# Attention of a one-core transformer kernel: projection blocks, sums of squares and key norms are placed anew over the steps

## Chip, cores and metric

The kernel runs as one program on one core of one Trainium2 chip. The metric is the device time of one execution in microseconds. The median of the runs counts.

## What is computed

The reference is a stack of two networks on one sequence of 512 tokens and 1024 channels. The first has two layers of convolution and retention. The second puts 16 meta tokens ahead (528 rows), runs a state-space layer and an MLP, then a multi-head latent attention (MLA) layer and an MLP. Only the MLA layer is touched:

```python
def mla_mixer(h, w_in, q_a_g, w_q_b, kv_a_g, w_kv_b, q_norm_g, k_norm_g, w_out):
    q_lat, kv_lat, k_pe = jnp.split(h @ w_in, [MLA_Q_RANK, MLA_Q_RANK + MLA_KV_RANK], axis=-1)
    q = (rms_norm_2(q_lat, q_a_g) @ w_q_b).reshape(bsz, L, MLA_HEADS, MLA_QK)
    kv = (rms_norm_2(kv_lat, kv_a_g) @ w_kv_b).reshape(bsz, L, MLA_HEADS, MLA_NOPE + MLA_V)
    k_nope, v = jnp.split(kv, [MLA_NOPE], axis=-1)
    k = jnp.concatenate([k_nope, k_pe of all heads], axis=-1)
    q = rms_norm_2(q, q_norm_g)
    k = rms_norm_2(k, k_norm_g)
    ...                                  # rotary turn of the last 32 of 96
    for s, e in blocks:                  # the 16 meta rows, then blocks of 128
        sc = jnp.einsum('bqhd,bkhd->bhqk', q[:, s:e], k[:, :e]) * scale
        p = jax.nn.softmax(jnp.where(mask, sc, -jnp.inf), axis=-1)
        outs.append(jnp.einsum('bhqk,bkhd->bqhd', p, v[:, :e]))
    return o @ w_out
```

There are 16 heads of 64 + 32 channels. Queries and keys are each divided by the root of their mean square (per head and token) before the scores.

## The kernel before

The code is written in one function for each engine, and each engine runs its instructions strictly in the order in which they are written. Engines meet only at semaphores (`wait_ge`). So the order of the calls in `pe_mla` (TensorE), `act_mla` (ScalarE) and `dve_mla` (VectorE) is the schedule.

The 16 heads are handled as 8 pairs, and a pair as 8 steps, `n` = 0 to 7: four query tiles of 128 tokens for head 0, then four for head 1. `STEPS` gives the tile order 0, 1, 3, 2, so that the scores of the four steps of a head have 144, 272, 528 and 400 key columns. The step counter over all pairs is `i`, 64 steps in all. Each step does:

- TensorE: the scores of step i with a mask matmul (`pe_scores`, L933 to L937), the transposes of the probabilities of step i-1 (`pe_turn_p`, L953, L955), and their product with V of step i-2 (`pe_times_v`, L970, L972, 64 columns each).
- VectorE: the maximum of each row of the scores and its negative, scaled (`dve_top`, L2258, L2260).
- ScalarE: the exponential (`act_exp`, L1426) and the copy of the transposed probabilities (`act_copy_pt`, L1439, L1441).

Beside the steps of a pair runs the preparation of the next two:

- Projection (`pe_pair_block`, L360): the queries and keys of a pair are a "unit" of 8 blocks of 128 x 128 weights. A block is three fp32r matmuls (high by high, low by high, high by low parts) of 512 columns; blocks 0 to 2 give the queries of head 0, 3 to 5 those of head 1, and 6 and 7, of two times 264 columns, the keys of both heads. They write banks 0, 1 and 2 to 3 of PSUM.
- `act_pair_q_squares`, `act_pair_keys`: squares of the queries, a copy of the keys with their gain (`k_raw`), squares of the keys (`k_squared`).
- Sums of squares (`pe_pair_totals`, L909, L913): four parts (two heads, two halves), each one 264-column fp32 matmul for the keys and two one-column ones for the queries, in banks 2 and 3.
- `dve_pair_mean` (L2214), `act_pair_rsqrt` (L1105, L1107: logarithm, then exponential) and three Newton parts (`dve_pair_newton`, L2225 to L2231) give the inverse roots of both heads in one tile of 1064 columns. `dve_pair_keys` (L2243, L2247) multiplies the keys of both heads by them and signals `k_done`; the first scores of the pair wait for it.
- `dve_pair_plain` (L2183) and `dve_pair_turn` (L2193, L2199, L2204) write the queries.

In the last two pairs there is no further pair to project, and blocks of the output projection stand as fillers in places named by `PLACES`. Weights come by DMA on SyncE's queue, are split on ScalarE (`act_split`) and GpSimd (`pool_low`, L340); that is not changed but for the step in which ScalarE splits.

In TensorE's loop before, the preparation sits like this:

```python
        if more and n == 2:
            pe_pair_totals(g, e, pair + 1, 0, 1)
        ...
        if project and n >= 4:
            pe_pair_block(g, e, pair + 2, (1, 2, 4, 6)[n - 4])
        ...
        if project and n == 2:
            pe_pair_block(g, e, pair + 2, 0)
        ...
        if project and n >= 5:
            pe_pair_block(g, e, pair + 2, (3, 5, 7)[n - 5])
```

## Time and profile before

| | us |
|---|---|
| median of 3 runs | 2783.66 |
| lowest, highest | 2774.49, 2784.95 |
| profiled execution | 2770.03 |
| its span, first to last instruction | 2768.2 |
| TensorE busy | 2672.4 (97%) |
| VectorE busy | 1223.6 (44%) |
| ScalarE busy | 980.4 (35%) |
| mean granted TensorE clock | 0.967 |

The attention loop runs from the first scores at 2092.5 us to the last transposes at 2365.5 us of the span. The page gives busy time by engine and, in 40 slices, the granted clock. The windows view gives for a stretch, in this order, its length, then busy time and number of instructions of TensorE, of its weight loads, of VectorE, ScalarE and GpSimd, then the granted clock (1.00 is 2.4 GHz, 0.50 is 1.2 GHz), DMA share and GB/s. The timeline gives instructions in order of time, those of one line merged, with the idle time before them and its releaser in brackets. Times and clocks of one execution stand beside a median of others, so small differences between the two mean nothing.

### The profile page before, as it was taken

Reading aid. Unit: us, or ns where it says so; the run is one execution under the profiler, and the core shown is the slowest. Engines: PE = TensorE matmul, PEld = TensorE weight load, DVE = VectorE, ACT = ScalarE, POOL = GpSimd, SP = SyncE. Lnnn points to the kernel's source line nnn. Section 1 sums busy time; section 2 is a strip of 40 time slices with the busy share of each in tenths; the row PEclk is TensorE's granted clock in tenths of the full one; section 3 lists DMA queues with packets and bytes.
Section 4 is the critical chain, followed back from the end, with each engine's and each line's share of the span. In section 5 each row is a group of like instructions: output and inputs, shape, how many; then the busy total and the mean of one; then the engine's idle time right before and its main releaser. Section 6 shows DMA issues by size and latency. Waiting matters only on the chain.

```text
span 2768.2 us, 36003 instructions
## 1 busy us (share of the span) xinstructions
PE 2672.4 (97%) x15144; PEld 2272.1 (82%) x15144; DVE 1223.6 (44%) x1649; ACT 980.4 (35%) x1479; POOL 932.2 (34%) x381
## 2 busy tenths in 40 slices
PE   7999999899999997999999999999979999999999
PEld 5777778677777777999999999999956777778887
DVE  6444442354444318688777331121244555422111
ACT  4333333433333323444444332232333444333222
POOL 3343344243443431233323334443321000254443
PEclk9999999999999998999999999999987888999999
DMA  4233332233332331221211222323210000133332
GB/s 134 86 111 93 95 109 84 62 110 93 95 101 86 101 91 39 62 62 56 62 60 58 73 84 86 94 88 92 81 54 23 24 16 15 55 107 99 92 91 92
DMA packets 61328, 215.65 MB, mean 78 GB/s; under 512 B 8176, under 2 KB 8560, under 8 KB 61168
## 3 DMA queue, kind: packets, MB, share of 16 engines
q1 hardware_dynamic: 57248, 202.05, 24.3%
q10 hardware_dynamic: 3920, 11.31, 1.3%
q8 instruction: 120, 1.97, 0.3%
q14 instruction: 40, 0.33, 0.0%
HBM read 211.24 MB, written 2.10 MB: 77 GB/s over the span
## 4 chain that ended last, share of the span: by engine, by line
PE 91%; DVE 5%; ACT 2%; issue 1%; DMA 0%; POOL 0%; ACTq 0%; DVEq 0%
PE psum L360 75%; PE psum L454 1%; PE psum L464 1%; PE psum L647 1%; PE psum L909 1%; PE psum L970 1%; PE psum L936 1%; PE psum L650 1%; PE psum L913 1%; PE psum L972 1%; PE psum L934 1%; PE psum L372 1%; PE psum L953 1%; PE psum L602 1%; DVE sb_scale L1537 1%
## 5 line engine op out<-in xcount | busy, mean ns | idle before, releaser
L340 POOL TENSOR_TENSOR sb_w_lo<-sb_w_raw,sb_w_hi 128x1024 fp32r<-128x1024 f32 x377 | 932.0, 2475 | 1813.9 <-ACT sb_w_hi L1098 1813.7
L360 PE MATMUL psum<-sb_h_hi,sb_w_hi 128*128 128x512 f32 (+1 forms) x2648 | 824.1, 353 | 48.2 <-DVE sb_h_lo L1546 32.7
L360 PE MATMUL psum<-sb_h_lo,sb_w_hi 128*128 128x512 f32 (+1 forms) x2648 | 795.5, 342 | 0.0
L360 PE MATMUL psum<-sb_h_hi,sb_w_lo 128*128 128x512 f32 (+1 forms) x2648 | 791.9, 341 | 0.0
L1098 ACT ACTIVATE sb_w_hi<-sb_w_raw 128x1024 fp32r<-128x1024 f32 x377 | 395.5, 1054 | 602.7 <-PE psum L360 458.8
L360 PEld LDWEIGHTS psum<-sb_h_hi,sb_w_hi 128*128 128x128 f32 x2648 | 459.5, 190 | 123.8 <-issue 36.5
L360 PEld LDWEIGHTS psum<-sb_h_lo,sb_w_hi 128*128 128x128 f32 x2648 | 458.1, 190 | 62.9 <-issue 7.5
L360 PEld LDWEIGHTS psum<-sb_h_hi,sb_w_lo 128*128 128x128 f32 x2648 | 458.4, 190 | 56.6
L360 PE MATMUL psum<-sb_mix_hi,sb_w_hi 128*128 128x264 f32 (+1 forms) x1424 | 421.9, 342 | 10.2 <-POOL sb_w_lo L340 5.6
L360 PE MATMUL psum<-sb_mix_lo,sb_w_hi 128*128 128x264 f32 (+1 forms) x1424 | 414.0, 336 | 0.0
L360 PE MATMUL psum<-sb_mix_hi,sb_w_lo 128*128 128x264 f32 (+1 forms) x1424 | 412.4, 335 | 0.0
L360 PEld LDWEIGHTS psum<-sb_mix_hi,sb_w_hi 128*128 128x128 f32 x1424 | 244.3, 190 | 48.2 <-issue 8.5
L360 PEld LDWEIGHTS psum<-sb_mix_hi,sb_w_lo 128*128 128x128 f32 x1424 | 243.9, 190 | 27.6
L360 PEld LDWEIGHTS psum<-sb_mix_lo,sb_w_hi 128*128 128x128 f32 x1424 | 244.1, 190 | 25.3 <-issue 0.5
L2114 DVE TENSOR_TENSOR sb_resid<-sb_resid,psum 128x528 f32<-128x528 f32 (+1 forms) x64 | 44.6, 697 | 289.9 <-PE psum L360 289.9
L2104 DVE SCALAR_TENSOR_TENSOR sb_square<-psum,sb_scale 128x528 f32<-128x528 f32 (+1 forms) x64 | 44.7, 699 | 174.9 <-PE psum L360 174.8
L1338 ACT ACTIVATE sb_scaled<-sb_square 128x528 f32<-128x528 f32 (+1 forms) x64 | 40.9, 639 | 216.6 <-DVE sb_square L2104 216.6
L1426 ACT ACTIVATE sb_p<-psum,sb_neg_top,sb_rinv 128x144 f32<-128x144 f32 (+1 forms) x64 | 40.4, 631 | 133.4 <-DVE sb_neg_top L2260 133.2
L2108 DVE TENSOR_TENSOR sb_mix_lo<-sb_scaled,sb_mix_hi 128x528 fp32r<-128x528 f32 (+1 forms) x64 | 49.0, 766 | 84.6 <-ACT sb_mix_hi L1340 84.6
L1546 DVE SCALAR_TENSOR_TENSOR sb_h_lo<-sb_resid,sb_cols,sb_h_hi 128x512 fp32r<-128x512 f32 (+1 forms) x48 | 51.7, 1078 | 49.1 <-ACT sb_h_hi L1114 48.8
L1272 ACT ACTIVATE sb_part<-psum,sb_neg_a 88x88 f32<-88x88 f32 x192 | 46.0, 329 | 67.9 <-PE psum L629 67.9
L1741 DVE TENSOR_TENSOR sb_ssq<-sb_ssq,sb_square 128x512 f32<-128x512 f32 x14 | 13.7, 979 | 127.0 <-ACT sb_square L1181 127.0
(275 smaller groups left out, 2637.7 us busy)
## 6 DMA issues: line engine op xcount, KB each, us to landing
sb_w_raw<-in_weights SPq DMA_DIRECT2D x377, 512.0 KB, 3.5
sb_decay<-in_decay ACTq DMA_DIRECT2D x16, 640.0 KB, 3.9
sb_resid<-in_x SPq DMA_DIRECT2D x4, 512.0 KB, 9.6
out<-sb_resid SPq DMA_DIRECT2D x8, 256.0 KB, 2.1
sb_table<-in_rope_table ACTq DMA_DIRECT2D x1, 264.0 KB, 3.4
sb_s<-in_positions ACTq DMA_DIRECT2D x1, 256.0 KB, 7.6
sb_cols<-in_cols ACTq DMA_DIRECT2D x1, 158.5 KB, 4.8
sb_ones<-in_ones ACTq DMA_DIRECT2D x1, 64.0 KB, 5.9
```

The source lines that it names most:

```text
L340: e.tensor_tensor(g.w_lo[:, u % 4, :], g.w_raw[:, u % 2, :], g.w_hi[:, u % 4, :].bitcast(F32), ALU.subtract).then_inc(S["w_lo"], 1)
L360: mm = e.matmul(g.psum[0:m, at + b, 0:wd], w[:, slot, P * i:P * i + m], xs[:, tile, c:c + wd], start=first and n == 0, stop=last and n == 2)
L372: mm = e.matmul(g.psum[:, 6 + b, 0:w], g.ones[:, :], g.square[:, m % 2, c:c + w], start=m == 0, stop=m == KT - 1)
L454: e.matmul(g.psum[:, 4 + j % 2, 0:WIDE1[j]], g.k[:, P * j:P * j + P], g.q[:, P * j:SEQ], start=True, stop=True).then_inc(S["scores"], 1)
L1098: e.activation(g.w_hi[:, u % 4, :], g.w_raw[:, u % 2, :], ACT.Copy).then_inc(S["w_hi"], 1)
L1272: a = e.activation(g.part[0:Q, h % 2, Q * j:Q * j + Q], g.flat(at + Q * j, Q)[0:Q], ACT.Exp, bias=g.neg_a[0:Q, j, n:n + 1])
L1338: e.activation(g.scaled[:, m % 2, c], g.square[:, m % 2, c], ACT.Square).then_inc(S["relu_sq"], 1)
L1426: e.activation(g.p[:, i % 2, 0:KEYS[t]], g.flat(at, KEYS[t]), ACT.Exp, bias=g.neg_top[:, n:n + 1], scale=g.q_scale(pair, h, t), accum_out= ...
L1546: e.scalar_tensor_tensor(g.h_lo[:, m, c], g.resid[:, m, c], g.gain(n, m), g.h_hi[:, m, c].bitcast(F32), ALU.mult, ALU.subtract).then_inc(S ...
L2104: e.scalar_tensor_tensor(part(g.square[:, m % 2, c]), product(k), 0.0, part(g.scale[:, c]), ALU.max, ALU.mult).then_inc(S["relu"], 1)
L2108: e.tensor_tensor(g.mix_lo[:, m, c], g.scaled[:, m % 2, c], g.mix_hi[:, m, c].bitcast(F32), ALU.subtract).then_inc(S["hidden"], 1)
L2114: e.tensor_tensor(r, r, product(k), ALU.add).then_inc(S["add"], 1)
```

## The change

Nothing in the arithmetic changes. The placement does:

- TensorE: every step of pairs 0 to 5 has one projection block. Blocks 0 to 5 of pair + 2 stand in steps 2 to 7, and blocks 6 and 7 in steps 0 and 1 of the pair after. The start-up does six blocks of pair 1, not eight. The four parts of the sums of squares stand at the ends of steps 3 to 6.
- Inverse roots and keys go head by head: the tiles of 1064 and 1056 columns are worked in halves of 532 and 528. Head 0 of the next pair is done in steps 5 to 7; head 1 has its mean and logarithm in step 7 and its Newton parts and keys in steps 2 and 3 of its own pair. `k_done` counts heads, and steps 0 and 4 both wait for it.
- ScalarE: the keys move from step 0 to step 2, with the squares first; the split moves from step 2 to step 1; the squares of the queries come after the exponential of step 7.
- VectorE: `dve_pair_plain` moves from step 7 to step 0 of the next pair.
- `PLACES`: 7 fillers in pair 6 (8 before), 14 in pair 7 (13 before).

```diff
@@ -92,8 +92,8 @@
-def rs_qk(pair):
-    return 34 + pair
+def rs_qk(pair, h):
+    return 34 + 2 * pair + h
@@ -885,7 +889,7 @@
     if i == 6 and pair:
-        e.wait_ge(S["mean"], rs_qk(pair - 1))
+        e.wait_ge(S["mean"], rs_qk(pair - 1, 1))
     c0, widths = (META, (SEQ,)) if i < 6 else (0, (HALF, HALF))
@@ -901,9 +905,9 @@
             e.wait_ge(S["q_squared"], pair + 1)
-            e.wait_ge(S["k_squared"], pair + 1)
+            e.wait_ge(S["k_raw"], 2 * pair + 2)
         else:
-            e.wait_ge(S["qk_mean"], pair + 1)
+            e.wait_ge(S["mean"], rs_qk(pair, 0))
     rows = slice(64 * h, 64 * h + 64)
@@ -921,8 +925,8 @@
     h, t, at = STEPS[n]
-    if n == 0:
-        e.wait_ge(S["k_done"], pair + 1)
+    if n % 4 == 0:
+        e.wait_ge(S["k_done"], 2 * pair + h + 1)
     if i == 0:
@@ -990,8 +994,8 @@
 FILLERS = [(m, n) for m in range(3) for n in range(PAIRS - 2)] + [(m, PAIRS - 2) for m in range(3)]
-PLACES = [(NS * (PAIRS - 2) + n, at) for n, at in ((2, 1), (4, 0), (5, 0), (5, 1), (6, 0), (6, 1), (7, 0), (7, 1))]
-PLACES += [(NS * (PAIRS - 1) + n, at) for n in range(1, NS) for at in range(2) if (n, at) != (4, 1)]
+PLACES = [(NS * (PAIRS - 2) + n, at) for n, at in ((2, 0), (3, 0), (4, 0), (5, 0), (6, 0), (7, 0), (7, 1))]
+PLACES += [(NS * (PAIRS - 1) + n, at) for n in range(NS) for at in range(2) if (n, at) not in ((0, 0), (4, 1))]
 FILL = dict(zip(PLACES, FILLERS))
@@ -1029,18 +1033,16 @@
             pe_pair_totals(g, e, 0, h, half)
-    for k in range(8):
+    for k in range(6):
         pe_pair_block(g, e, 1, k)
...
         pe_scores(g, e, i)
-        if more and n == 2:
-            pe_pair_totals(g, e, pair + 1, 0, 1)
-        if more and n == 3:
-            pe_pair_totals(g, e, pair + 1, 1, 0)
-        if project and n >= 4:
-            pe_pair_block(g, e, pair + 2, (1, 2, 4, 6)[n - 4])
+        if more and n < 2:
+            pe_pair_block(g, e, pair + 1, 6 + n)
+        if project and n >= 2:
+            pe_pair_block(g, e, pair + 2, n - 2)
         if (i, 0) in FILL:
@@ -1048,16 +1050,10 @@
             pe_times_v(g, e, i - 2)
-        if more and n == 1:
-            pe_pair_totals(g, e, pair + 1, 0, 0)
-        if more and n == 3:
-            pe_pair_totals(g, e, pair + 1, 1, 1)
-        if project and n == 2:
-            pe_pair_block(g, e, pair + 2, 0)
+        if more and 3 <= n < 7:
+            pe_pair_totals(g, e, pair + 1, (n - 3) // 2, (n - 3) % 2)
         if pair and n == 2:
             pe_out_turn(g, e, pair - 1)
-        if project and n >= 5:
-            pe_pair_block(g, e, pair + 2, (3, 5, 7)[n - 5])
         if (i, 1) in FILL:
@@ -1399,20 +1395,21 @@
     e.wait_ge(S["unit"], U_PAIRS[pair] + 1)
+    if pair == 0:
+        e.wait_ge(S["kpe_total"], 1)
+    else:
+        e.wait_ge(S["qk_total"], 2 * pair)
+    e.activation(halves(g.ksq[:, :]), g.both(2), ACT.Square).then_inc(S["k_squared"], 1)
     if pair >= 2:
...
                      scale=g.col("k_norm", 1, rows)).then_inc(S["k_raw"], 1)
-    if pair == 0:
-        e.wait_ge(S["kpe_total"], 1)
-    e.activation(halves(g.ksq[:, :]), g.both(2), ACT.Square).then_inc(S["k_squared"], 1)
-def act_pair_rsqrt(g, e, pair):
-    e.wait_ge(g.S["qk_mean"], pair + 1)
-    act_rsqrt(g, e, rs_qk(pair), g.mean2[:, :], g.rinv2[pair % 2][:, :])
+def act_pair_rsqrt(g, e, pair, h):
+    act_rsqrt(g, e, rs_qk(pair, h), g.norms(g.mean2, h), g.norms(g.rinv2[pair % 2], h))
@@ -1455,26 +1452,29 @@
     act_split(g, e, U_PAIRS[1] + LEAD)
-    act_pair_rsqrt(g, e, 0)
+    for h in range(2):
+        act_pair_rsqrt(g, e, 0, h)
     act_pair_q_squares(g, e, 1)
...
         pair, n = divmod(i, NS)
-        if pair + 2 < PAIRS and n == 7:
-            act_pair_q_squares(g, e, pair + 2)
         act_exp(g, e, i)
...
         if pair + 1 < PAIRS:
-            if n == 0:
+            if n == 1 and pair:
+                act_split(g, e, U_PAIRS[pair + 1] + LEAD)
+            if n == 2:
                 act_pair_keys(g, e, pair + 1)
-            if n == 2 and pair:
-                act_split(g, e, U_PAIRS[pair + 1] + LEAD)
-            if n == 4:
-                act_pair_rsqrt(g, e, pair + 1)
+            if n == 5:
+                act_pair_rsqrt(g, e, pair + 1, 0)
         elif n == 2:
...
             act_pair_out(g, e, pair - 1)
+        if pair + 2 < PAIRS and n == 7:
+            act_pair_q_squares(g, e, pair + 2)
+        if pair + 1 < PAIRS and n == 7:
+            act_pair_rsqrt(g, e, pair + 1, 1)
     act_copy_pt(g, e, ALL_STEPS - 1)
@@ -2210,16 +2210,15 @@
     if pair:
-        e.wait_ge(S["newton"], 3 * rs_qk(pair - 1))
-    e.tensor_tensor(g.mean2[:, 2 * QK_HALF * h:2 * QK_HALF * (h + 1)].rearrange("p (a c) -> p a c", a=2),
-                    g.psum[:, 2:4, 0:QK_HALF], g.kpe_part[:, :, :],
-                    ALU.add).then_inc(S["mean" if h else "qk_mean"], 1)
-def dve_pair_newton(g, e, pair, part):
-    S = g.S
-    n = rs_qk(pair)
-    mean, y, t = g.mean2[:, :], g.rinv2[pair % 2][:, :], g.newton2[:, :]
+        e.wait_ge(S["newton"], 3 * rs_qk(pair - 1, h))
+    e.tensor_tensor(g.norms(g.mean2, h).rearrange("p (a c) -> p a c", a=2), g.psum[:, 2:4, 0:QK_HALF],
+                    g.kpe_part[:, :, :], ALU.add).then_inc(S["mean"], 1)
+def dve_pair_newton(g, e, pair, h, part):
+    S = g.S
+    n = rs_qk(pair, h)
+    mean, y, t = (g.norms(to, h) for to in (g.mean2, g.rinv2[pair % 2], g.newton2))
     if part == 0:
@@ -2231,20 +2230,20 @@
-def dve_pair_keys(g, e, pair, part):
-    S = g.S
-    r = g.rinv2[pair % 2][:, :].rearrange("p (h a c) -> p h a c", h=2, a=2)
-    k = g.k2[:, pair % 2, :, :].rearrange("p h (a c) -> p h a c", a=2)
+def dve_pair_keys(g, e, pair, h, part):
+    S = g.S
+    r = g.norms(g.rinv2[pair % 2], h).rearrange("p (a c) -> p a c", a=2)
+    k = halves(g.k2[:, pair % 2, h, :])
     if part == 0:
-        e.wait_ge(S["newton"], 3 * rs_qk(pair))
+        e.wait_ge(S["newton"], 3 * rs_qk(pair, h))
         if pair >= 2:
             e.wait_ge(S["scores2"], NS * (pair - 1))
-        e.tensor_tensor(k[64:96], halves(g.kpe[64:96, :]).unsqueeze(1).to_broadcast([32, 2, 2, HALF]),
-                        r[64:96, :, :, 0:HALF], ALU.mult).then_inc(S["k_rot2"], 1)
+        e.tensor_tensor(k[64:96], halves(g.kpe[64:96, :]), r[64:96, :, 0:HALF],
+                        ALU.mult).then_inc(S["k_rot2"], 1)
     else:
-        e.wait_ge(S["k_raw"], 2 * pair + 2)
-        e.tensor_tensor(k[0:64], k[0:64], r[0:64, :, :, 0:HALF], ALU.mult).then_inc(S["k_done"], 1)
+        e.wait_ge(S["k_raw"], 2 * pair + h + 1)
+        e.tensor_tensor(k[0:64], k[0:64], r[0:64, :, 0:HALF], ALU.mult).then_inc(S["k_done"], 1)
@@ -2291,33 +2290,36 @@
     for part in range(3):
-        dve_pair_newton(g, e, 0, part)
-    dve_pair_keys(g, e, 0, 0)
-    dve_pair_keys(g, e, 0, 1)
-    dve_pair_plain(g, e, 1)
+        dve_pair_newton(g, e, 0, 0, part)
+    for part in range(2):
+        dve_pair_keys(g, e, 0, 0, part)
     for i in range(ALL_STEPS):
...
             if n == 0:
+                dve_pair_plain(g, e, pair + 1)
                 dve_pair_turn(g, e, pair + 1, 0)
...
             if n == 2:
+                dve_pair_turn(g, e, pair + 1, 2)
+            if n == 5:
                 dve_pair_mean(g, e, pair + 1, 0)
-                dve_pair_turn(g, e, pair + 1, 2)
-            if n == 3:
+            if n == 6:
+                for part in range(3):
+                    dve_pair_newton(g, e, pair + 1, 0, part)
+            if n == 7:
                 dve_pair_mean(g, e, pair + 1, 1)
-            if n == 5:
-                dve_pair_newton(g, e, pair + 1, 0)
-                dve_pair_newton(g, e, pair + 1, 1)
-            if n == 6:
-                dve_pair_newton(g, e, pair + 1, 2)
-                dve_pair_keys(g, e, pair + 1, 0)
-            if n == 7:
-                dve_pair_keys(g, e, pair + 1, 1)
-        if pair + 2 < PAIRS and n == 7:
-            dve_pair_plain(g, e, pair + 2)
+                dve_pair_keys(g, e, pair + 1, 0, 0)
+                dve_pair_keys(g, e, pair + 1, 0, 1)
+        if n == 2:
+            dve_pair_newton(g, e, pair, 1, 0)
+            dve_pair_newton(g, e, pair, 1, 1)
+        if n == 3:
+            dve_pair_newton(g, e, pair, 1, 2)
+            dve_pair_keys(g, e, pair, 1, 0)
+            dve_pair_keys(g, e, pair, 1, 1)
         if n == 1 and pair:
...
         if n == 4 and pair:
```

The row numbers of the order views below are lines of each version. First, TensorE in step 1 of pair 2, from its scores to the next step's; before (L360 would be a block, L909 and L913 are sums of squares):

```order
L936 MATMUL psum<-sb_k_116,sb_q_115 128x272 [waits s_exp2]
L937 MATMUL psum<-sb_mask,sb_ident_60 128x128
L953 MATMUL psum<-sb_ident,sb_p 128x128 [waits s_pt,s_exp2]
L955 MATMUL psum<-sb_ident,sb_p 16x128
L970 MATMUL psum<-sb_v_all,sb_pt 128x64 [waits s_pt]
L970 MATMUL psum<-sb_v_all,sb_pt 128x64 x2
L972 MATMUL psum<-sb_v_all,sb_pt 128x64
L909 MATMUL psum<-sb_ksq,sb_ones 128x264 [waits s_k_squared,s_q_squared]
L913 MATMUL psum<-sb_ones,sb_square 128x1 x2
L933 MATMUL psum<-sb_k_116,sb_q_115 128x16 [waits s_exp2]
```

After:

```order
L940 MATMUL psum<-sb_k_116,sb_q_115 128x272 [waits s_exp2]
L941 MATMUL psum<-sb_mask,sb_ident_60 128x128
L364 MATMUL psum<-sb_mix_hi,sb_w_hi 128x264 x2
L364 MATMUL psum<-sb_mix_lo,sb_w_hi 128x264 x2
L364 MATMUL psum<-sb_mix_hi,sb_w_lo 128x264 x2
L957 MATMUL psum<-sb_ident,sb_p 128x128 [waits s_pt,s_exp2]
L959 MATMUL psum<-sb_ident,sb_p 16x128
L974 MATMUL psum<-sb_v_all,sb_pt 128x64 [waits s_pt]
L974 MATMUL psum<-sb_v_all,sb_pt 128x64 x2
L976 MATMUL psum<-sb_v_all,sb_pt 128x64
L937 MATMUL psum<-sb_k_116,sb_q_115 128x16 [waits s_exp2]
```

The sums of squares are gone from the step's end, and a block (L364, three times two matmuls of 264 columns) stands behind the scores.

Second, VectorE in step 7 of pair 2 and the start of step 0 of pair 3, before:

```order
L2258 TENSOR_REDUCE sb_top<-psum 128x1 [waits s_exp2,s_scores2]
L2260 SCALAR_TENSOR_TENSOR sb_neg_top<-sb_top,sb_rinv_0_112 128x1 [waits s_top_raw]
L2247 TENSOR_TENSOR sb_k_116<-sb_k_116,sb_rinv_1_113 64x1056 [waits s_k_raw]
L2183 TENSOR_SCALAR sb_q_115<-psum,sb_cols 64x1024 [waits s_scores2,s_q_squared]
L2258 TENSOR_REDUCE sb_top<-psum 128x1 [waits s_exp2,s_scores2]
L2260 SCALAR_TENSOR_TENSOR sb_neg_top<-sb_top,sb_rinv_1_113 128x1 [waits s_top_raw]
L2193 SCALAR_TENSOR_TENSOR sb_q_115<-psum,sb_cols,sb_table 32x1024
```

After (the first two rows are the maximum of step 7, L2214 is the mean of head 1, L2242 and L2246 the keys of head 0):

```order
L2257 TENSOR_REDUCE sb_top<-psum 128x1 [waits s_exp2,s_scores2]
L2259 SCALAR_TENSOR_TENSOR sb_neg_top<-sb_top,sb_rinv_0_112 128x1 [waits s_top_raw]
L2214 TENSOR_TENSOR sb_mean_110<-psum,sb_kpe_part 128x532 [waits s_newton,s_kpe_part,s_qk_total]
L2242 TENSOR_TENSOR sb_k_116<-sb_kpe,sb_rinv_1_113 32x528 [waits s_scores2,s_newton]
L2246 TENSOR_TENSOR sb_k_116<-sb_k_116,sb_rinv_1_113 64x528 [waits s_k_raw]
L2257 TENSOR_REDUCE sb_top<-psum 128x1 [waits s_exp2,s_scores2]
L2259 SCALAR_TENSOR_TENSOR sb_neg_top<-sb_top,sb_rinv_1_113 128x1 [waits s_top_raw]
L2183 TENSOR_SCALAR sb_q_115<-psum,sb_cols 64x1024 [waits s_scores2,s_q_squared]
L2193 SCALAR_TENSOR_TENSOR sb_q_115<-psum,sb_cols,sb_table 32x1024
```

The mean now stands ahead of the keys, which are half as wide, and the plain queries (L2183) have moved behind the maximum of step 0.

Third, VectorE in step 3 of pair 3, before:

```order
L2258 TENSOR_REDUCE sb_top<-psum 128x1 [waits s_exp2,s_scores2]
L2260 SCALAR_TENSOR_TENSOR sb_neg_top<-sb_top,sb_rinv_1_113 128x1 [waits s_top_raw]
L2214 TENSOR_TENSOR sb_mean_110<-psum,sb_kpe_part 128x532 [waits s_newton,s_kpe_part,s_qk_total]
L2258 TENSOR_REDUCE sb_top<-psum 128x1 [waits s_exp2,s_scores2]
L2260 SCALAR_TENSOR_TENSOR sb_neg_top<-sb_top,sb_rinv_1_113 128x1 [waits s_top_raw]
```

After (L2230 is the last Newton part, L2242 and L2246 are the keys of head 1 of the pair itself):

```order
L2257 TENSOR_REDUCE sb_top<-psum 128x1 [waits s_exp2,s_scores2]
L2259 SCALAR_TENSOR_TENSOR sb_neg_top<-sb_top,sb_rinv_1_113 128x1 [waits s_top_raw]
L2230 SCALAR_TENSOR_TENSOR sb_rinv_1_113<-sb_newton_111,sb_rinv_1_113 128x532 [waits s_newton]
L2242 TENSOR_TENSOR sb_k_116<-sb_kpe,sb_rinv_1_113 32x528 [waits s_scores2,s_newton]
L2246 TENSOR_TENSOR sb_k_116<-sb_k_116,sb_rinv_1_113 64x528 [waits s_k_raw]
L2257 TENSOR_REDUCE sb_top<-psum 128x1 [waits s_exp2,s_scores2]
L2259 SCALAR_TENSOR_TENSOR sb_neg_top<-sb_top,sb_rinv_1_113 128x1 [waits s_top_raw]
```

The mean is gone and half a Newton part and half the keys stand there, ahead of the maximum of step 4.

## Rows read from the trace of the kernel before

**Rows 1.** The page, part 2: granted TensorE clock in 40 slices, tenths
```profile
PEclk9999999999999998999999999999987888999999
```

**Rows 2.** Windows, pairs 0 to 7 of the attention; columns as the first line says
```profile
core 0: us, PE busy (x) PEld busy (x) DVE busy (x) ACT busy (x) POOL busy (x), PEclk, DMA share, GB/s
2092.50:2130.22 37.72, 35.32 (x144) 25.37 (x145) 18.85 (x30) 14.16 (x31) 0.00 (x0) 0.68 0.00 1
2130.22:2164.61 34.39, 34.24 (x172) 25.68 (x171) 19.56 (x33) 16.00 (x34) 2.35 (x1) 0.80 0.06 16
2164.61:2197.44 32.83, 32.68 (x173) 24.58 (x171) 19.49 (x33) 15.84 (x34) 2.35 (x1) 0.84 0.06 17
2197.44:2236.49 39.05, 38.90 (x173) 29.50 (x172) 19.62 (x33) 16.17 (x34) 2.35 (x1) 0.69 0.04 14
2236.49:2264.53 28.04, 27.89 (x172) 21.69 (x171) 20.17 (x33) 15.61 (x34) 2.35 (x1) 1.00 0.07 20
2264.53:2300.47 35.94, 35.78 (x173) 27.46 (x172) 19.46 (x33) 16.06 (x34) 2.36 (x1) 0.76 0.05 15
2300.47:2337.88 37.41, 37.27 (x167) 27.66 (x166) 18.80 (x32) 15.04 (x33) 2.36 (x1) 0.73 0.05 15
2337.88:2365.47 27.59, 27.04 (x156) 21.06 (x155) 8.34 (x21) 10.86 (x28) 2.35 (x1) 1.00 0.07 20
```

**Rows 3.** Windows, steps 3 and 4 of pair 3, then of pair 4
```profile
2210.23:2223.82 13.59, 13.59 (x47) 10.04 (x47) 2.51 (x6) 4.64 (x10) 0.74 (x1) 0.50 0.12 39
2246.37:2253.70 7.33, 7.33 (x49) 5.59 (x47) 3.10 (x6) 3.42 (x9) 2.35 (x1) 1.00 0.26 72
```

**Rows 4.** Windows of 2 us in pairs 1, 3 and 5
```profile
2134.00:2136.00 2.00, 1.85 (x11) 1.40 (x11) 1.64 (x3) 1.20 (x4) 0.00 (x0) 0.88 0.04 8
...
2204.00:2206.00 2.00, 2.00 (x8) 1.19 (x7) 0.87 (x2) 0.82 (x2) 0.00 (x0) 0.50 0.04 8
...
2272.00:2274.00 2.00, 2.00 (x11) 1.77 (x10) 1.56 (x3) 1.62 (x4) 0.00 (x0) 0.52 0.00 0
```

**Rows 5.** Timeline of TensorE in pair 4: start us, us, engine, line, operation
```profile
2243.05 0.71 PE L909 MATMUL psum<-sb_ksq,sb_ones 64*128 64x264 f32 x2
...
2244.16 0.41 PE L953 MATMUL psum<-sb_ident,sb_p 128*128 128x128 f32 x2
...
2254.29 0.48 PE L360 MATMUL psum<-sb_mix_hi,sb_w_hi 128*128 128x512 f32 x1
...
2255.06 0.27 PE L953 MATMUL psum<-sb_ident,sb_p 128*128 128x128 f32 x1
...
2258.23 0.22 PE L937 MATMUL psum<-sb_mask,sb_ident 128*128 128x128 bf16 x1
...
2262.30 0.60 PE L953 MATMUL psum<-sb_ident,sb_p 128*128 128x128 f32 x4
...
2263.69 0.51 PE L360 MATMUL psum<-sb_mix_hi,sb_w_hi 128*128 128x264 f32 x2
```

**Rows 6.** Timeline of VectorE in pair 4
```profile
2251.01 0.71 DVE L2214 TENSOR_TENSOR sb_mean<-psum,sb_kpe_part 128x532 f32<-128x532 f32 x1 [2.26 <-PE psum L913]
...
2258.49 0.71 DVE L2258 TENSOR_REDUCE sb_top<-psum 128x1 f32<-128x528 f32 x1
...
2261.88 0.57 DVE L2258 TENSOR_REDUCE sb_top<-psum 128x1 f32<-128x400 f32 x1
...
2262.57 1.25 DVE L2247 TENSOR_TENSOR sb_k<-sb_k,sb_rinv 64x1056 f32<-64x1056 f32 x1
```

**Rows 7.** Timeline, end of the start-up: VectorE, then TensorE [idle before <-releaser]
```profile
2082.96 0.71 DVE L2214 TENSOR_TENSOR sb_mean<-psum,sb_kpe_part 128x532 f32<-128x532 f32 x1 [3.38 <-PE psum L913]
...
2091.19 1.25 DVE L2247 TENSOR_TENSOR sb_k<-sb_k,sb_rinv 64x1056 f32<-64x1056 f32 x1
...
2089.31 0.41 PE L360 MATMUL psum<-sb_mix_hi,sb_w_hi 128*128 128x264 f32 x2
...
2092.50 0.51 PE L936 MATMUL psum<-sb_k,sb_q 96*128 96x144 f32 x2 [1.58 <-DVE sb_k L2247]
...
2094.70 0.48 PE L953 MATMUL psum<-sb_ident,sb_p 128*128 128x128 f32 x1 [1.06 <-ACT sb_p L1426]
```

8 lines of the change are left out of this document (5 added, 3 removed).

## Prediction

> **What bounds the kernel now.** First the page: TensorE is busy over nearly the whole span, and its granted clock is at or near full except in the slices of the attention [rows 1]. So I read that stretch pair by pair, by a table of windows that run from the first scores of a pair to the first scores of the next [rows 2]. TensorE is busy in all but 0.15 us of most of them, yet the same work takes between 28.0 and 39.1 us. What differs is the clock. Pair 4 is at 1.00 throughout and takes 28.04 us; pair 3 has a mean of 0.69 and takes 39.05 us. There are two levels, 2.4 and 1.2 GHz, so a mean of 0.69 over 39.05 us is 2 x 0.31 x 39.05 = 24.2 us at the lower one. The same sum gives 24.1, 13.8, 10.5, 24.2, 0, 17.3, 20.2 and 0 us for pairs 0 to 7: 110.1 us at 1.2 GHz.
>
> The price of one such microsecond is read from one piece of work done at either level: steps 3 and 4 take 13.59 us at 0.50 in pair 3 and 7.33 us at 1.00 in pair 4 [rows 3]. So 6.26/13.59 = 0.46 us is lost for each microsecond at the lower clock. Check: pairs 1, 2, 3 and 5 are together 30.1 us over four times 28.04, and 0.46 x 65.8 us is 30.3. In all, 110.1 x 0.46 = 50.6 us of the attention is the clock's. Waits of TensorE are little beside that.
>
> Where the clock falls is the next thing to see: in three 2-us windows it has just gone down at 2135.5, 2204 and 2272 us [rows 4], which is 5.3, 6.5 and 7.5 us after the first scores of pairs 1, 3 and 5. Ahead of that lie steps 0 and 1, the only steps in which TensorE has no projection block: it runs scores, transposes, the small products with V and the first sums of squares. It is busy there, but much of it is 64-column and one-column matmuls. Pair 7, with a filler block in every step from 1 on, keeps 1.00; pair 4, in the same order as its neighbours, keeps it too [rows 2]. So the thin stretch is a near thing, not a certainty.
>
> **The change part by part.** TensorE has the same matmuls as before; none is added or removed.
>
> (a) The blocks. Steps 0 and 1 get a block each and steps 2 to 7 one each, where before steps 5 to 7 had two and steps 0, 1 and 3 none. The sums of squares (1.1 us for each part, from its first matmul to the work behind it [rows 5]) leave steps 1 to 3, where four of them stood around three scores, and stand one each at the ends of steps 3 to 6. The stretch that precedes each fall is thereby filled, and what is thinned was the densest. I expect the lower clock to become rare, not to vanish: pair 0 still starts behind waits, and one later spell is likely enough. I put 22 us at 1.2 GHz in place of 110, two spells like the shorter ones now (10.5 and 13.8 us). That leaves 22 x 0.46 = 10.1 of the 50.6 us. The bounds are 0 us and all 110 us.
>
> The Trainium skill, "TensorE: Matmul & The Clock Gate", section "HAM oscillation — how this bites in real kernels", gives idle gaps of TensorE as what brings the clock down. The trace does not bear this out for these falls: TensorE is idle for 0.15 us in all in each of pairs 1, 3 and 5 [rows 2]. What the rule would make of the change is rival C.
>
> (b) A new wait at step 0. The scores of a pair's first head wait for its keys (`k_done`), and on VectorE these are now finished in step 7 behind that step's maximum and the mean of head 1. Count from the mask matmul that ends a step's scores. VectorE starts the maximum 0.26 us later (2258.23 to 2258.49) [rows 5, 6]; maximum and its small follower take 0.69 [rows 6]; the mean of 532 columns takes 0.71 [rows 6], and I give each of the two key multiplies, now 528 wide, the same 0.71 (at 1056 they take 1.25 [rows 6]). That is 3.1 us less some overlap, say 3.0. TensorE in the same time has a block (2254.29 to 2255.06, 0.77), and transposes and V product of step 7 (2262.30 to 2263.69, 1.39) [rows 5]: 2.2 us. So the scores wait 0.8 us where before a second block (0.8 us) covered it. Seven pair boundaries: 7 x 0.8 = +5.6 us; bounds 3 and 8.
>
> (c) The second head's keys are asked for at step 4. VectorE in step 3 does a maximum, one Newton part and two key multiplies: 0.69 + 3 x 0.71 = 2.8, after a step 2 with the 528-wide maximum, a 1.25 us rotation sum and two Newton parts, 3.6 us against about 3.0 of TensorE work behind step 2's scores. TensorE behind step 3's scores has a block of 0.77, transposes and V product of about 1.39 and sums of 1.1 [rows 5]: 3.3 us. The two are level, 2.8 + 0.6 against 3.3. I take +0.5 us for all pairs; bounds 0 and +4 (0.5 us a pair). Queued behind this wait is all of TensorE.
>
> (d) ScalarE. Squares come ahead of the key copies and all of it in step 2; sums need it only at the end of step 3, so it is covered. Logarithm and exponential in two halves are two more instructions a pair on an engine that is busy 16 of 28 us [rows 2]: nothing. VectorE's five more instructions, each at about 0.17 us of fixed cost (2 x 0.71 less 1.25 [rows 6]), lie in its idle time but for what (b) and (c) count.
>
> (e) The start. Before, the first scores wait for the keys: TensorE starts at 2092.50 after 1.58 us idle, with VectorE's second key multiply starting at 2091.19 [rows 7]. After, six blocks stand ahead, which end where block 6 starts now, at 2089.3; VectorE has only head 0 to finish, from the end of the second mean (2083.7) three Newton parts and two multiplies of 0.71, done at 2087.3 [rows 7]. So the scores start 3.2 us earlier. The two blocks return in steps 0 and 1 (+1.6) and cover the 1.06 us wait seen there now [rows 7]; against that, `dve_pair_plain` and both rotations of pair 1 (about 1.25 us each) now stand ahead of block 0 of pair 2, whose wait is some 2 us in pair 0 only. I take -2 us; bounds -4 and +1.
>
> Tail: the fillers move by one place between pairs 6 and 7; nothing waits for that, 0.
>
> **Sum**, on the profiled execution: 2770.0 - 50.6 + 10.1 + 5.6 + 0.5 - 2 = 2733.6 us. The median of before is 13.6 us above that execution, and the four times shown differ by 15. Part of this is, I take it, more or fewer low-clock spells in the very stretch that the change fills, and would go with them. I carry a third: 2738 us.
>
> **The rivals.**
> A, the forecast: 2738.
> B, the new waits of (b) and (c) are themselves thin places, next to the one-column matmuls, and about half of the lower clock stays: 55 us, 25.3 lost. 2770.0 - 25.3 + 4.1 + 4.4 = 2753. For it: pair 4 shows that the margin is small, and a 0.8 us hole now stands ahead of step 0.
> C, the placing of blocks does not move the clock at all: it falls by idle gaps elsewhere or by chance. Then only the waits remain, 2770.0 + 4.1 = 2774, and up to 2788 against the median. Within half a per cent. Against it: three falls at nearly the same place of the pair [rows 4], with next to no idle time ahead of them [rows 2]. The rule of idle gaps of the Trainium skill's page "TensorE: Matmul & The Clock Gate", section "HAM oscillation — how this bites in real kernels", would give this same result, since the change takes out no such gap.
> D, slower. Once down, the clock now returns in the pairs before step 5 or in it, where two blocks a step begin; pair 3 stayed low through its steps 3 and 4, which hold one block between them [rows 3]. If an even mixture of one block a step is enough to keep the clock but too thin to bring it back, each fall lasts for pairs. It costs 0.46 a microsecond: over the median from 110 + (13.6 - 4.1)/0.46 = 131 us of low clock in 273; with 190 us, 2770 + 36.8 + 4.1 = 2811. Against it: pair 2 came back with 10.5 us low, so before its dense steps.
>
> **How the numbers follow.** Half a per cent (14 us) is about what a measurement of this kernel can tell from no change. A 0.60, B 0.20, C 0.12, D 0.08. A and B are faster by more than half a per cent (below 2769.7), C is within it, D mostly slower. Faster 0.80, same 0.14, slower 0.06. The range goes from no low clock at all with small waits (2770.0 - 50.6 + 0.6 = 2720) to the edge of C, 2769.
>
> **What would show it.** Right: pairs 1 to 5 at a clock of 0.95 or more and 28.5 to 29.5 us each; a wait of 0.5 to 1 us ahead of a pair's first scores with the key multiply as releaser; first scores about 3 us earlier. Wrong in (a): pairs still of 33 to 39 us with means of 0.7 to 0.8, then by where the clock falls it is B (behind step 0's wait) or C (anywhere), and by spells over 25 us it is D. Wrong in (b) or (c): pairs at full clock over 30 us.

## The result, and the profile after

The changed kernel takes 2742.4 us, the median of four runs (2741.21 to 2752.84); the kernel before, on the same chip, 2783.97 (2774.49 to 2784.95). The ratio is 0.9867, with a 95% interval of 0.9834 to 0.9899; here and below a ratio is that of the means of the runs, so that it can differ by some tenths of a per cent from that of the medians. The forecast was 2738 us. The profiled execution took 2742.57 us, against 2770.03 before: 27.5 us less, where the sum had 36.4 less.

First the granted clock of TensorE on the page, 40 slices in tenths. [rows 1] has 87888 there; the last four of these slices are the attention, the first lies ahead of it. Now it has 88, of which the second is the first slice of the attention:

```profile
PEclk9999999999999998999999999999988999999999
```

Then the eight pairs, from the first scores of one to the first scores of the next, to be laid beside [rows 2]:

```profile
core 0: us, PE busy (x) PEld busy (x) DVE busy (x) ACT busy (x) POOL busy (x), PEclk, DMA share, GB/s
2090.49:2120.40 29.91, 26.36 (x146) 19.37 (x144) 19.14 (x34) 13.55 (x32) 0.00 (x0) 0.94 0.00 1
2120.40:2154.18 33.78, 32.89 (x171) 25.09 (x171) 21.06 (x37) 15.78 (x37) 2.36 (x1) 0.85 0.06 16
2154.18:2184.22 30.04, 28.21 (x171) 21.84 (x170) 21.06 (x37) 16.09 (x37) 2.36 (x1) 1.00 0.05 18
2184.22:2214.29 30.07, 28.24 (x170) 21.84 (x171) 21.06 (x37) 15.88 (x37) 2.36 (x1) 1.00 0.06 18
2214.29:2245.93 31.64, 29.82 (x170) 23.18 (x170) 21.07 (x37) 15.87 (x37) 2.36 (x1) 0.95 0.05 18
2245.93:2275.99 30.06, 28.25 (x171) 21.86 (x171) 21.04 (x37) 15.87 (x37) 2.35 (x1) 1.00 0.06 19
2275.99:2307.65 31.66, 30.73 (x173) 23.61 (x173) 21.07 (x37) 15.85 (x38) 2.36 (x1) 0.95 0.06 18
2307.65:2337.02 29.37, 28.17 (x161) 22.04 (x162) 11.69 (x26) 11.32 (x29) 2.35 (x1) 1.00 0.07 19
```

Two things are to be seen. The clock: by the sum of the prediction, 2 x (1 - clock) x length, these pairs hold 20.1 us at 1.2 GHz, where those before held 110.1 (the clocks have two digits, so such a sum is good to about 1 us). And the second column, TensorE's busy time, is no longer nearly the whole window: at full clock a pair has 30.05 us with 28.22 busy, where pair 4 before had 28.04 with 27.89. Over all eight pairs TensorE is idle for 13.9 us (246.5 less 232.65 busy) where it was idle for 3.9 (273.0 less 269.1).

What it waits for is listed by the waits of TensorE from 2090 to 2337 us: what waits, for whom, us in total, times, longest.

```profile
PE psum L940 <- DVE sb_k L2246: 8.1, 12, 1.2
PE psum L940 <- ACT sb_p L1423: 3.1, 6, 0.5
PE psum L937 <- ACT sb_p L1423: 2.5, 1, 2.5
```

These are four kinds of places. In the order of the timeline of TensorE (start us, us, line, operation, [idle before <-releaser]): step 2 of pair 0; step 3 and step 4, here of pair 2; step 0, here of pair 3.

```profile
2095.75 0.41 PE L937 MATMUL psum<-sb_k,sb_q 96*128 96x16 f32 x2 [2.50 <-ACT sb_p L1423]
...
2163.90 0.94 PE L940 MATMUL psum<-sb_k,sb_q 96*128 96x400 f32 x2 [0.52 <-ACT sb_p L1423]
...
2168.49 0.51 PE L940 MATMUL psum<-sb_k,sb_q 96*128 96x144 f32 x2 [0.37 <-DVE sb_k L2246]
...
2184.22 0.51 PE L940 MATMUL psum<-sb_k,sb_q 96*128 96x144 f32 x2 [0.94 <-DVE sb_k L2246]
```

The last is the wait of (b); it stands at the start of pairs 1, 3, 4, 5 and 6, five times 0.94 us. Ahead of pair 2 TensorE is at low clock and so later itself, and ahead of pair 7 fillers cover it. The one before it is that of (c), 0.37 us in each of pairs 1 to 6, and 1.20 us in pair 7. The first, 2.50 us, comes from VectorE: the plain queries and the first rotation of pair 1, 1.28 us each, stand between the maxima of steps 0 and 1, and behind them come the exponential of step 1 and the scores of step 2. The wait of 0.52 us in step 3, in pairs 1 to 6 too, was not foreseen. Its chain is seen in the timeline of the other engines, just ahead of it:

```profile
2160.55 2.36 POOL L344 TENSOR_TENSOR sb_w_lo<-sb_w_raw,sb_w_hi 128x1024 fp32r<-128x1024 f32 x1 [31.41 <-ACT sb_w_hi L1094]
...
2161.22 0.71 DVE L2257 TENSOR_REDUCE sb_top<-psum 128x1 f32<-128x528 f32 x1 [0.68 <-PE psum L941]
...
2161.97 0.96 DVE L2259 SCALAR_TENSOR_TENSOR sb_neg_top<-sb_top,sb_rinv 128x1 f32<-128x1 f32 x1
...
2162.96 0.79 ACT L1423 ACTIVATE sb_p<-psum,sb_neg_top,sb_rinv 128x528 f32<-128x528 f32 x1 [2.49 <-DVE sb_neg_top L2259]
```

`sb_neg_top` is one column and takes 0.16 us as a rule. Here it takes 0.96, as in the other five of pairs 1 to 6 (0.94 to 0.96), and ends at 2162.93, as GpSimd's split (`w_lo`) ends at 2162.91. The exponential of step 2 waits for it, and the scores of step 3 for the exponential, since they take its bank. In pair 4 before, at full clock too, the split ran in step 3; the change calls `act_split` in step 1, and so GpSimd's half falls into step 2. The Trainium skill, "GPSIMD Engine Reference", section "1. Specifications", has it that GpSimd shares its SBUF interface with VectorE, in contention with instructions of VectorE that have two SBUF inputs. This trace agrees: `neg_top` has two, `sb_top` and `sb_rinv`, and is held for 0.8 us.

### The profile page after: what moved, and what is told of

It reads as the page before. It is cut to its first block, busy times and chain, and to the rows that moved or that the text cites. A ratio compares the mean times of both kernels' runs of the same rounds, so it can differ in the third digit from the quotient of the medians.

```text
span 2740.8 us, 36067 instructions
## 1 busy us (share of the span) xinstructions
PE 2635.8 (96%) x15144; PEld 2248.0 (82%) x15144; DVE 1229.7 (45%) x1689; ACT 980.4 (36%) x1495; POOL 931.5 (34%) x381
## 4 chain that ended last, share of the span: by engine, by line
PE 90%; DVE 7%; ACT 1%; issue 1%; DMA 0%; POOL 0%; DVEq 0%; ACTq 0%
PE psum L364 75%; PE psum L458 1%; PE psum L468 1%; PE psum L651 1%; PE psum L974 1%; PE psum L654 1%; PE psum L940 1%; PE psum L913 1%; PE psum L606 1%; PE psum L938 1%; PE psum L376 1%; PE psum L976 1%; PE psum L917 1%; PE psum L665 1%; DVE sb_scale L1537 1%
## 5 line engine op out<-in xcount | busy, mean ns | idle before, releaser
L364 PE MATMUL psum<-sb_h_hi,sb_w_hi 128*128 128x512 f32 (+1 forms) x2648 | 822.3, 352 | 48.6 <-DVE sb_h_lo L1546 32.3
L364 PE MATMUL psum<-sb_h_lo,sb_w_hi 128*128 128x512 f32 (+1 forms) x2648 | 794.4, 341 | 0.0
L364 PE MATMUL psum<-sb_h_hi,sb_w_lo 128*128 128x512 f32 (+1 forms) x2648 | 790.9, 340 | 0.0
L364 PEld LDWEIGHTS psum<-sb_h_hi,sb_w_hi 128*128 128x128 f32 x2648 | 459.0, 190 | 124.2 <-issue 35.6
L364 PEld LDWEIGHTS psum<-sb_h_lo,sb_w_hi 128*128 128x128 f32 x2648 | 457.7, 190 | 62.4 <-issue 7.0
L364 PEld LDWEIGHTS psum<-sb_h_hi,sb_w_lo 128*128 128x128 f32 x2648 | 457.9, 190 | 56.2
L364 PE MATMUL psum<-sb_mix_hi,sb_w_hi 128*128 128x264 f32 (+1 forms) x1424 | 420.8, 341 | 10.2 <-POOL sb_w_lo L344 5.6
L364 PE MATMUL psum<-sb_mix_lo,sb_w_hi 128*128 128x264 f32 (+1 forms) x1424 | 413.7, 336 | 0.0
L364 PE MATMUL psum<-sb_mix_hi,sb_w_lo 128*128 128x264 f32 (+1 forms) x1424 | 412.5, 335 | 0.0
L364 PEld LDWEIGHTS psum<-sb_mix_hi,sb_w_hi 128*128 128x128 f32 x1424 | 244.7, 190 | 51.7 <-issue 12.8
L364 PEld LDWEIGHTS psum<-sb_mix_hi,sb_w_lo 128*128 128x128 f32 x1424 | 244.1, 190 | 27.5
L364 PEld LDWEIGHTS psum<-sb_mix_lo,sb_w_hi 128*128 128x128 f32 x1424 | 244.3, 190 | 25.6 <-issue 0.5
L2104 DVE SCALAR_TENSOR_TENSOR sb_square<-psum,sb_scale 128x528 f32<-128x528 f32 (+1 forms) x64 | 44.7, 698 | 175.0 <-PE psum L364 174.9
```

The source lines that it names most:

```text
L364: mm = e.matmul(g.psum[0:m, at + b, 0:wd], w[:, slot, P * i:P * i + m], xs[:, tile, c:c + wd], start=first and n == 0, stop=last and n == 2)
L2104: e.scalar_tensor_tensor(part(g.square[:, m % 2, c]), product(k), 0.0, part(g.scale[:, c]), ALU.max, ALU.mult).then_inc(S["relu"], 1)
```

## What was to be told apart

The size of (a) came out almost as forecast, and this proves nothing of its cause. The change did three things to TensorE's order at once: it put blocks in steps 0, 1 and 3, spread the sums of squares from steps 1 to 3 over steps 3 to 6, and took second blocks out of steps 5 to 7. It also moved work on the other engines. The prediction's theory was that the thin steps 0 and 1 bring the clock down (thin: busy with transposes, 64-column and one-column matmuls, and no block). Its rivals were idle gaps (C), and that the placing is not what matters. And one question comes from the result: do the 1.8 us of waits in each pair cost what they take?

Eleven kernels were run, in three groups; every ratio is to the kernel before on the same chip. "Low clock" is time at 1.2 GHz, worked out as above over the attention of the profiled execution; a "fall" is where it starts. One microsecond of it costs 0.46 us [rows 3].

One execution can mislead here. Seven of the profiled executions below run pair 0 in one and the same order up to step 3 (all of the last two groups but the one with blocks ahead in 0 and 4, and the changed kernel above), and yet four have 3 us of low clock in it and three have 10. The mean granted clock over the whole span is known of every run. In the fourteen profiled executions 68 to 87 us of low clock lie outside the attention, so 2 x (1 - clock) x span less 78 us is an estimate of the low clock in the attention of any run, good to some 10 us. It is given where the profiled execution is not a typical one.

## Experiments on where the clock falls

**Extra work in the thin steps.** The kernel before, with six matmuls of 352 columns ahead of the scores in steps 0 and 1. Their results are overwritten by the scores, so this is work added, none left out.

```diff
@@ pe_scores, of the kernel before
+    if n < 2:
+        bank = 4 if n == 0 else 5
+        for _ in range(6):
+            e.matmul(g.psum[:, bank, 0:352], g.mix_hi[:, 0, META:META + P],
+                     g.mix_hi[:, 1, META:META + 352], start=True, stop=True)
```

> The kernel before, with six extra fp32r matmuls of 352 columns ahead of the scores of steps 0 and 1 of every pair (their result is overwritten by the scores). That is 6 x 352 / 2.4 GHz = 0.88 us a step, 1.76 a pair, 14 us of work that nothing needs. Theory (the clock falls because steps 0 and 1 hold no dense work): most of the 110 us at 1.2 GHz go, so 0.46 x 90 = 41 us are won and 14 paid: about 27 us below the kernel before (2755 against 2784), pairs 1 to 5 near 30 us each. Rival (the change won by where sums and keys stand, or by its earlier start, and blocks in steps 0 and 1 have no part in the clock): 10 to 20 us slower than before, clock of the pairs still 0.7 to 0.85.

Measured: 2768.74 us (before 2772.49), ratio 0.9985, 0.9963 to 1.0007. These are 96 matmuls of 0.147 us (a full-clock pair takes 29.80 us for 28.04, with twelve more), 14 us of work, at no cost in time. That is neither the 27 us faster of the theory nor the 10 to 20 us slower of the rival. The clock did not come back as the theory had it: pairs 0 to 6 hold 92.3 us of low clock in the profiled execution (2774.92 us, clock 0.970), and by the estimate about 70 in the median one (0.973). Pairs 3 and 4, the columns as above:

```profile
2200.40:2239.62 39.22, 39.22 (x183) 30.38 (x183) 19.48 (x32) 16.04 (x34) 2.35 (x1) 0.74 0.04 14
2239.62:2269.42 29.80, 29.80 (x184) 23.61 (x183) 20.14 (x32) 15.61 (x34) 2.35 (x1) 1.00 0.06 18
```

Two readings. TensorE is busy for 39.22 of 39.22 us and is at a mean clock of 0.74 all the same, so no idle gap that the profile shows brings the clock down here (the ends of matmuls are modelled in it, and it would not show tiny gaps between them). The Trainium skill, "TensorE: Matmul & The Clock Gate", section "HAM oscillation — how this bites in real kernels", gives idle gaps of TensorE as the cause; for these falls the measurement decides against it. And the falls have moved on a little: in pairs 1, 2, 3, 5 and 6 the first one comes 1.6 to 2.8 us behind the first scores of step 2, where before it came from 0.4 us ahead of them to 2.3 us behind. What stands there are the sums of squares, ahead of the scores and behind them, transposes and small products with V. In windows of 1 us in pair 2:

```profile
2174.00:2175.00 1.00, 1.00 (x4) 0.30 (x3) 0.10 (x1) 0.00 (x0) 0.00 (x0) 1.00 0.00 0
2175.00:2176.00 1.00, 1.00 (x4) 0.35 (x3) 0.77 (x2) 0.17 (x1) 0.00 (x0) 0.54 0.00 0
```

So it looks as if steps 0 and 1 are a part of the thin stretch and not the whole; that is what the kernel with steps 0 to 3 filled asks.

**The same work in the dense steps.** The condition is `n >= 6` instead of `n < 2`.

> The twin of the run before: the same extra matmuls, ahead of the scores of steps 6 and 7, which hold two projection blocks each anyway. Theory: steps 0 to 3 stay as thin as they are, so the clock falls as in the kernel before, and the 14 us are paid: 2790 to 2800 us, pair means of 0.7 to 0.85. Rival (any extra TensorE work, wherever it stands, holds the clock): as fast as the run before.

Measured: 2803.34 us, ratio 1.0104, 1.0073 to 1.0135; low clock 102.5 us in pairs 0 to 6. But the profiled execution, 2782.81 us at a clock of 0.967, is the fastest of six; the four slowest, from 2801 us up, have clocks of 0.959 to 0.962, by the estimate some 135 to 150 us of low clock. That explains the two levels: 0.008 of the clock is some 45 us at 1.2 GHz, or 21 us of time. The same 96 matmuls cost 31 us here and -4 us there by the medians. Where work stands is worth 35 us; how much of it there is, 14.

**Extra work in steps 0 to 3.** The condition is `n < 4`: 192 extra matmuls, 28 us at full clock.

> The kernel before with six extra 352-column matmuls ahead of the scores in each of steps 0 to 3 (their results are overwritten by the scores), where c1_fill_thin_steps had them in steps 0 and 1 alone: 32 x 0.88 = 28 us more work at full clock. Theory (the falls come from steps 0 to 3 as a whole, since four scores, three or four sums of squares and one block stand there): low clock from 92 us to 30 us or less, no falls at step 2, so 2770 + 28 - 0.46 x 80 = 2761 us, not above the kernel before. Rival (steps 2 and 3 do not matter, or the clock falls without regard to what stands there): low clock stays at 90 us or more, time 2783 us or more.

Measured: 2759.17 us (before 2769.5), ratio 0.9955, 0.9927 to 0.9982. Pairs 1 to 3:

```profile
2123.28:2156.62 33.34, 33.34 (x196) 26.86 (x196) 19.41 (x32) 15.97 (x34) 2.37 (x1) 0.95 0.05 16
2156.62:2188.35 31.73, 31.73 (x196) 25.52 (x195) 19.50 (x32) 15.75 (x34) 2.36 (x1) 1.00 0.05 18
2188.35:2221.72 33.37, 33.37 (x197) 26.82 (x196) 19.40 (x32) 15.97 (x34) 2.36 (x1) 0.95 0.05 16
```

Low clock is 13 us in the profiled execution, from 110, and no fall is left in step 2; what is left of pairs 1 to 6 are three falls of 3 us at the start of step 4, the step behind the filled ones. A kernel with 28 us more of useless multiplication is 10 us faster (5 to 20 by the interval). This is the test that carries (a): the clock falls by what stands in steps 0 to 3, and work that fills them mostly holds it, with nothing else of the change made. Steps 2 and 3 were not filled alone, so their share is not known, nor which property of the small matmuls counts. The profiled execution, 2751.31 us, is near the fast end of twelve (2751.05 to 2771.99). Six of them are at clocks of 0.983 to 0.985 like it, and six, from 2763 us up, at 0.977 to 0.981, which is 17 to 39 us more of low clock; even so less than before.

**The changed kernel with its blocks of steps 0 and 1 put in step 2.** The sums stay spread. Step 2 then holds three blocks.

```diff
-        if more and n < 2:
-            pe_pair_block(g, e, pair + 1, 6 + n)
+        if more and n == 2:
+            pe_pair_block(g, e, pair + 1, 6)
+            pe_pair_block(g, e, pair + 1, 7)
```

> The changed kernel, with blocks 6 and 7 both at step 2 in place of one in step 0 and one in step 1. Steps 0 and 1 then hold no block, as before the change, but no sums of squares either. Theory: the low clock comes back in part, 40 to 80 us of it against 20 in the changed kernel: 2752 to 2770 us. Rival (it is the sums of squares of steps 1 to 3 that pulled the clock down, and moving them was enough): about 20 us of low clock and 2742 us, as the changed kernel.

Measured: 2746.67 us, ratio 0.9905, 0.9883 to 0.9926; low clock 43.3 us, with one fall in each of the pairs 0 to 6, all in steps 0 and 1 or in the first 1.2 us of step 2. Four of the seven last some 7 us. Pairs 2 and 4:

```profile
2152.36:2184.17 31.81, 30.87 (x170) 23.87 (x170) 20.35 (x37) 15.88 (x37) 2.35 (x1) 0.89 0.06 18
...
2216.89:2248.05 31.16, 29.30 (x171) 23.15 (x171) 21.57 (x37) 15.88 (x37) 2.37 (x1) 0.95 0.06 18
```

Taking the blocks out of steps 0 and 1 alone brings the falls back to just there, but short ones. The low clock is at the lower end of what the theory said and the time is below it; against the changed kernel (0.9867 and 0.9889) this ratio is 4 to 11 us behind, with overlapping intervals. So the blocks of steps 0 and 1 by themselves are worth little as long as the sums are spread and step 2 is full.

**The changed kernel with all its blocks where they were before.** The sums are still spread, keys and roots head by head. One block differs from before: block 6 stands at the end of step 7 and not behind its scores.

```diff
-    for k in range(6):
+    for k in range(8):
         pe_pair_block(g, e, 1, k)
...
-        if more and n < 2:
-            pe_pair_block(g, e, pair + 1, 6 + n)
-        if project and n >= 2:
-            pe_pair_block(g, e, pair + 2, n - 2)
+        if project and 4 <= n < 7:
+            pe_pair_block(g, e, pair + 2, (1, 2, 4)[n - 4])
...
+        if project and n == 2:
+            pe_pair_block(g, e, pair + 2, 0)
+        if project and 5 <= n < 7:
+            pe_pair_block(g, e, pair + 2, (3, 5)[n - 5])
+        if project and n == 7:
+            pe_pair_block(g, e, pair + 2, 6)
+            pe_pair_block(g, e, pair + 2, 7)
```

> The changed kernel with all blocks back in the places of the kernel before (0 in step 2, 1 in 4, then two a step in 5, 6 and 7, eight in the start-up); sums of squares, roots and keys stay as changed. Theory: steps 0, 1 and 3 are without a block again, the low clock is back at 80 to 110 us, and the new waits of 2 us a pair stay: 2775 to 2795 us, no faster than the kernel before. Rival (the gain is that of the new places of sums, roots and keys): 2742 to 2750 us.

Measured: 2760.75 us (2756.08 to 2777.5, ten runs), ratio 0.9964, 0.9942 to 0.9987. Pairs 1 to 3 each hold two falls, at step 2 + 0.6 to 0.7 us and at step 4 + 0.6 to 0.7 us, 7 and 3 us long; a wait of 0.9 us for ScalarE stands ahead of the first. Pair 4 has one of 30 us, and low clock is 98.8 us in this execution, 2771.92 us long, which is one of the slower of the ten; at the median clock, 0.9725, the estimate is about 75. Pairs 2 and 3:

```profile
2159.44:2193.53 34.09, 32.60 (x172) 25.00 (x171) 21.00 (x37) 15.76 (x38) 2.34 (x1) 0.85 0.05 16
2193.53:2227.57 34.04, 32.60 (x172) 25.06 (x171) 21.04 (x37) 15.75 (x38) 2.35 (x1) 0.85 0.05 16
```

The changed kernel stands at 0.9867 above and at 0.9889 in its repeat below, and so 0.0075 to 0.0097 of 2772 us under this one: the block places bring 21 to 27 us, the rest of the change, with the sums spread, some 10 (4 to 16 by the interval). The time lies between the 2775 us and more of the theory and the 2742 to 2750 of the rival: the block places are the greater part, not the whole.

## Experiments on the waits

These ask whether the waits that the change made can be had back. The changed kernel was run again beside them.

> The changed kernel once more, beside the three runs that follow, on the same chip: 0.985 to 0.99 of the kernel before; in its attention loop about 20 us at the lower clock, pairs 2, 3 and 5 near 30.05 us.

Measured: 2746.22 us (before 2770.78), ratio 0.9889, 0.985 to 0.9928; pairs at full clock of 30.05 us again, low clock 24.5 us in pairs 0, 4 and 6, the last two both at step 4 + 0.8 us.

**The split in step 4.** GpSimd's half then lies behind step 4's maximum.

```diff
-            if n == 1 and pair:
-                act_split(g, e, U_PAIRS[pair + 1] + LEAD)
             if n == 2:
                 act_pair_keys(g, e, pair + 1)
+            if n == 4 and pair:
+                act_split(g, e, U_PAIRS[pair + 1] + LEAD)
```

> The changed kernel with ScalarE's split of a weight unit in step 4 in place of step 1. Theory: GpSimd's part of the split (2.36 us) runs from step 1 into step 2 and holds up VectorE's small scaling of the 528-wide maximum (0.96 us for 0.16), which makes TensorE wait 0.52 us for the exponential at step 3 and 0.37 us for the keys at step 4; in step 4 there is slack for it. Both waits go in 6 pairs: pairs at full clock 29.2 us in place of 30.05, about 5 us faster than the changed kernel. Rival (VectorE is simply full in steps 0 to 3, and the long scaling is no contention): both waits stay, no difference.

Measured: 2752.03 us, ratio 0.9909, 0.9872 to 0.9946. What was asked of GpSimd is plain. `neg_top` of step 2 is back at 0.16 us, the wait of 0.52 is gone from the list, and a pair takes 29.25 us for 30.05, 0.5 of it by this wait. The wait of 0.37 us for the second head's keys, which was to go as well, stays at 0.34 to 0.37: it does not come from the collision. Timeline of VectorE in pair 2, then pairs 3 and 4 as windows:

```profile
2160.65 0.71 DVE L2257 TENSOR_REDUCE sb_top<-psum 128x1 f32<-128x528 f32 x1 [0.69 <-PE psum L941]
2161.39 0.16 DVE L2259 SCALAR_TENSOR_TENSOR sb_neg_top<-sb_top,sb_rinv 128x1 f32<-128x1 f32 x1
```

```profile
2182.84:2212.09 29.25, 27.96 (x171) 21.83 (x171) 20.59 (x37) 15.90 (x37) 2.36 (x1) 1.00 0.07 19
2212.09:2249.26 37.17, 35.89 (x170) 27.24 (x170) 20.26 (x37) 16.11 (x37) 2.34 (x1) 0.77 0.05 15
```

But low clock is 44.7 us for 20 to 25, from two falls at step 4 of 17 us each and one of 10 us in pair 0, and the gain is gone.

**The keys ahead of the mean.** Head 0's rotation sum moves to step 6, and its last multiply stands ahead of the mean in step 7.

```diff
                     dve_pair_newton(g, e, pair + 1, 0, part)
+                dve_pair_keys(g, e, pair + 1, 0, 0)
             if n == 7:
-                dve_pair_mean(g, e, pair + 1, 1)
-                dve_pair_keys(g, e, pair + 1, 0, 0)
                 dve_pair_keys(g, e, pair + 1, 0, 1)
+                dve_pair_mean(g, e, pair + 1, 1)
```

> The changed kernel with the first key multiply of head 0 in step 6 and the second ahead of head 1's mean in step 7. Theory: the 0.94 us wait at each pair's first scores is the mean and one multiply in the chain behind the last maximum; it goes at 7 boundaries: full-clock pairs 29.1 us, about 6.6 us faster than the changed kernel. Rival: the wait comes back one place further, at block 6, which needs that mean: no difference.

Measured: 2745.22 us, ratio 0.9885, 0.9842 to 0.9927; full-clock pairs of 29.6 us, where 29.1 was expected. The wait of 0.94 at step 0 is gone, one of 0.5 for ScalarE's `sb_pt` has come, and low clock is 47.8 us, mostly from two falls at step 4 of 17 us. The median clock of its runs, 0.979, is that of the changed kernel's (0.9795), so that this much more low clock is shown for one execution alone.

**Both.**

> Both edits. Theory: the two add up, full-clock pairs at 28.1 to 28.3 us as in pair 4 of the kernel before, 11 to 12 us faster than the changed kernel (0.982 of before where that is 0.987), the low clock 20 us or less. Rival: what one edit gives is eaten by the other's wait: no more than 6 us.

Measured: 2748.3 us, ratio 0.989, 0.9851 to 0.993; full-clock pairs of 28.80 us, where 28.1 to 28.3 was expected, since the waits of 0.5 at step 0 and 0.35 at step 4 are left; low clock 51.0 us. Pairs 5 and 6:

```profile
2239.66:2268.46 28.80, 27.93 (x170) 21.83 (x171) 20.46 (x37) 15.79 (x37) 2.36 (x1) 1.00 0.07 19
2268.46:2303.84 35.38, 35.02 (x174) 27.04 (x174) 20.13 (x37) 17.04 (x38) 2.36 (x1) 0.81 0.06 16
```

The pair is shorter in all three, by what was expected only in the first, and the total is not. In the profiled executions 0.5 to 1.25 us in each of six pairs is more than given back by 25 to 31 us more of low clock than the changed kernel's 20.1, which is 11 to 14 us. The medians, 2752, 2745 and 2748 us beside 2746 for the changed kernel on the same chip, say the same of the other executions: none shows the 3 to 7.5 us that the shorter pairs would give at an equal clock. For the split and for both edits the clocks of all runs bear it out (median 0.976 for 0.9795, some 20 us more at 1.2 GHz); for the keys they do not, and the 3 us that it should give are within the scatter. Why a shorter wait elsewhere should lengthen the spells at step 4 was not settled. Where they start is common to all: in the kernels of this group, outside pair 0, ten of twelve falls in the attention come 0.4 to 1.2 us into step 4; the two others come in step 6 of the last kernel.

## Experiments on step 4

Ahead of a fall at step 4 stand transposes and V product of step 3, its sums with four one-column matmuls, and the narrowest scores (144 columns); the block of step 3 ended some 3 us before, and that of step 4 comes behind the scores. These three kernels put the block ahead of the scores: the first in step 4 alone, the second in steps 0 and 4 (`n in (0, 4)`), the third in step 4 of the kernel with both moves.

```diff
-        pe_scores(g, e, i)
-        if more and n < 2:
-            pe_pair_block(g, e, pair + 1, 6 + n)
-        if project and n >= 2:
-            pe_pair_block(g, e, pair + 2, n - 2)
+        first = n in (4,)
+        for part in range(2):
+            if part == first:
+                pe_scores(g, e, i)
+            elif more and n < 2:
+                pe_pair_block(g, e, pair + 1, 6 + n)
+            elif project and n >= 2:
+                pe_pair_block(g, e, pair + 2, n - 2)
```

> The changed kernel with one move: in step 4 of every pair the projection block stands ahead of the scores instead of behind them. The same matmuls. Theory (what is left of the clock's falls comes from the stretch made of step 3's V product and sums and step 4's narrow scores, because it holds no block): filling it removes the falls at step 4 + 0.4 to 1.3 us, low clock in the attention 0 to 10 us instead of 20 to 25, and the block also covers the 0.37 us wait for the second head's keys: pairs of 29.7 us at full clock, time about 2736 us (0.46 x 15 us and 6 x 0.37 us less than 2744). Rival (the falls only move, to wherever the thinnest place then is, as behind step 4's scores or at step 0): low clock stays at 20 to 45 us, falls at another step, 2742 to 2750 us.

Measured: 2733.37 us (2728.06 to 2738.02, six runs; before 2769.5), ratio 0.9852, 0.982 to 0.9884. Pairs 0, 4 and 5, and one step of TensorE's timeline:

```profile
2090.62:2120.22 29.60, 26.17 (x146) 19.28 (x144) 19.14 (x34) 13.55 (x32) 0.00 (x0) 0.94 0.00 1
...
2208.64:2238.11 29.47, 28.02 (x170) 21.79 (x170) 21.05 (x37) 15.79 (x37) 2.36 (x1) 1.00 0.06 19
2238.11:2267.58 29.47, 28.01 (x171) 21.78 (x171) 21.07 (x37) 15.80 (x37) 2.36 (x1) 1.00 0.06 19
```

```profile
2192.50 0.61 PE L917 MATMUL psum<-sb_ones,sb_square 96*128 96x1 f32 x4
2192.97 0.48 PE L364 MATMUL psum<-sb_mix_hi,sb_w_hi 128*128 128x512 f32 x1
...
2193.76 0.41 PE L940 MATMUL psum<-sb_k,sb_q 96*128 96x144 f32 x2
```

No fall is left in pairs 1 to 7. The only one in the attention is that of pair 0, 3.6 us. The scores of step 4 start without a wait in pairs 1 to 5, since the block covers the 0.37 us, and a pair takes 29.47 us. This is the theory's result in all its parts, to 3 us in time. One thing it does not separate: the move fills the thin stretch and takes away the wait of 0.37 us in the same place. That the thin stretch is enough by itself is what the kernel with steps 0 to 3 filled suggests, in which the clock falls at step 4 with no wait at all. All six runs lie below all ten of the changed kernel (2741.21 to 2752.84, on two other chips). The intervals of the ratios, 0.982 to 0.9884 and 0.9834 to 0.9899, overlap, so that it is about 10 us faster than the changed kernel is what the runs point to and not proved to the half per cent.

> The changed kernel with the block ahead of the scores in steps 0 and 4, so that both waits for keys (0.94 us at step 0 and 0.37 us at step 4 of each pair) have a block over them; the same matmuls. Theory (block placing decides both clock and waits): pairs at full clock of 28.9 to 29.2 us instead of 30.05, low clock 0 to 10 us, time about 2731 us. Rival (each wait taken out comes back as low clock, as in the kernels that move the split or the keys): pairs of 29 us at full clock but 40 us or more at the lower clock, 2742 to 2750 us.

Measured: 2735.83 us, ratio 0.9865, 0.9831 to 0.9898. No fall in pairs 1 to 7 again; low clock 10.4 us, all in pair 0. The wait for the keys at step 0 is gone, but a pair is hardly shorter: 29.40 us for 29.47. It waits in step 3 instead. A pair, and the wait in the pair before it:

```profile
2211.70:2241.10 29.40, 28.23 (x171) 21.79 (x171) 21.55 (x37) 15.69 (x37) 2.38 (x1) 1.00 0.06 19
```

```profile
2191.95 0.60 PE L940 MATMUL psum<-sb_k,sb_q 96*128 96x400 f32 x1 [0.99 <-ACT sb_p L1426]
```

The expected 28.9 to 29.2 us did not come, as the scores of step 3 wait for the exponential of step 2 and the collision with GpSimd's split, which now holds `neg_top` for 1.45 us in all; what the block covers at step 0 is waited for there. It shows also that over 1 us of idle time in every pair does not bring the clock down by itself: seven pairs in a row at 1.00.

> The kernel in which the split stands in step 4 and the keys ahead of the mean (28.8 us a pair at full clock, but 51 us at the lower clock, falls at steps 4 and 6), with the block of step 4 ahead of its scores. Theory (the falls at step 4 come from the thin stretch around its scores): falls at step 4 gone, low clock 20 us or less, time about 2734 us (0.46 x 31 us less than 2748). Rival (falls move to another place): low clock 40 us or more, time 2745 to 2750 us.

Measured: 2737.1 us, ratio 0.9869, 0.9833 to 0.9905. The falls at step 4 are gone and the pairs are the shortest of the group, but three falls have come at step 6, and low clock is 31.1 us. Pairs 2 and 5:

```profile
2149.72:2178.35 28.63, 27.80 (x171) 21.76 (x171) 20.91 (x37) 15.69 (x37) 2.36 (x1) 1.00 0.07 20
...
2238.49:2271.07 32.58, 32.25 (x170) 24.75 (x170) 20.92 (x37) 16.17 (x37) 2.36 (x1) 0.85 0.05 17
```

Theory and rival are each half right: filling step 4 took its falls and 20 us of low clock away, and then falls come at step 6, 0.4 to 1.7 us into it. Why there was not looked into.

The kernels of the last two groups side by side, with the median over the runs of each one's granted clock:

```
kernel                       pair at     low clock   profiled     median      median
                             full clock  attention   execution    time        clock
before                         28.04       110.1      2770.03     2770-2784   0.967
changed                        30.05        20.1      2742.57     2742.4      0.982
changed, again                 30.05        24.5      2741.87     2746.2      0.9795
split in step 4                29.25        44.7      2747.94     2752.0      0.976
keys ahead of mean             29.6         47.8      2746.05     2745.2      0.979
both                           28.80        51.0      2748.09     2748.3      0.976
block ahead in 4               29.47         3.6      2732.56     2733.4      0.984
blocks ahead in 0 and 4        29.40        10.4      2735.57     2735.8      0.983
both, block ahead in 4         28.63        31.1      2737.08     2737.1      0.981
```

The price of 0.46 carries from row to row. From "changed" to "both": 30.9 us more of low clock are 14.2, six pairs shorter by 1.25 are -7.5, first scores 1.3 us earlier; together +5.4, measured +5.5. From "changed" to "block ahead in 4": -7.6, five pairs shorter by 0.58 are -2.9, pair 0 is 0.3 shorter; together -10.8, measured -10.0.

## Why the prediction was right, point by point

**(a) The clock.** Right in size: 22 us of low clock forecast, 20.1 measured, -40.5 us forecast and 90 x 0.46 = -41.4 found. That it is right to 2 us is luck: 22 was a guess of two spells, and by their clocks other runs of the same kernel have up to 20 us more. The cause that it named was too narrow. That was steps 0 and 1, called the only ones without a block; step 3 had none either. Filling steps 0 and 1 alone left 92 us of low clock, and filling steps 0 to 3 left 13. The prediction's other half sentence, that four sums around three scores leave steps 1 to 3, mattered beside the blocks. The reading of [rows 4] was that a fall follows what stands ahead of it; what stood ahead reached into step 2 as well, and by that the falls in step 2 of the first experiment would have been foreseen. The spells left lie at step 4 and step 6, and in pair 0, which the forecast had named.

**(b) The wait at step 0.** 0.8 us forecast, 0.94 found, released by the key multiply as foreseen. It comes at five boundaries and not at seven, 4.7 us in all for 5.6. The count along VectorE in step 7 holds; what was left out is that low clock ahead of a boundary, and fillers, can hide such a wait.

**(c) The second head's keys.** Under-sized: "level" was 0.37 us behind in each of six pairs and 1.20 us in pair 7, 3.4 us where 0.5 was taken, inside the bounds of 0 to 4. (b) and (c) together are 8.1 us of waits for 6.1.

**(d) Work on the other engines costed at nothing.** This is the term that was wrong in its mechanism. ScalarE itself is covered, as said. But `act_split` was moved too, from step 2 to step 1, and with it GpSimd's 2.36 us, from a step where a slow `neg_top` was rare and hidden (it took 0.83 us in pair 4 before, ending with GpSimd's instruction and with no wait behind it, and 0.16 in the other pairs) to one where it is not: 0.52 us in each of six pairs, 3.1 us. Of a moved step every instruction counts on every engine; the prediction followed ScalarE and not GpSimd.

**(e) The start.** The first scores are 2.0 us earlier in this execution, not 3.2. In nine executions with this start-up they come from 2086.62 to 2091.54 us, with a mean of 2089.4, 3.1 us ahead of the 2092.50 before: on average the forecast holds, and the 1.2 us missing are this execution's. Behind them a wait of 2.50 us for ScalarE's `sb_p` stands in pair 0 where 1.06 was: the prediction charged `dve_pair_plain` and the rotations to a later block, and they hold up the maximum of step 1. The two blocks now in the loop take 1.6, and a wait of 1.34 us for the squares of the keys, which pair 0 had before, is gone. In sum -0.3 us where -2 was taken.

**The sum.** 27.5 us were gained on the profiled execution instead of 36.4. The 8.9 between are (a) -0.9, (b) and (c) +2.0, (d) +3.1, (e) +1.7, and +1.0 behind the attention, where this execution has 6.8 us of low clock at the start of the next stage and the one before had 3.4; the repeat of the changed kernel had 3.4 too, so this is no part of the change. Some 2.0 are left, and they are TensorE's busy time of 28.22 for 27.89 us in each of six pairs, which the prediction took as unchanged. The 4.4 us carried for the gap between profiled execution and median were not found: the changed kernel's profiled execution is at its median. So two errors of opposite sign, +8.9 and -4.6, left the forecast 4.4 us low; that it came this close is in part luck.

**The tests it set.** Pairs of 28.5 to 29.5 us were asked for, and those at full clock take 30.05; "wrong in (b) or (c): pairs at full clock over 30 us" is what the table shows, and the greater part of the excess is (d) and (c). Of pairs 1 to 5 four are at 0.95 or more and one at 0.85.

**The rivals.** B, half the low clock stays, was not the result. The kernels with blocks late or as before have about that much, but its mechanism, that the new waits are what brings the clock down, is not borne out: with the wait of 0.94 us at step 0 in place and one block moved, pairs 1 to 7 are at 1.00, and without it low clock was no less. C fell by the result, and its idle gaps by two things more: by 72 us of low clock in pairs 1 to 6 of the first experiment, without any idle time, and by seven pairs at 1.00 with an idle microsecond in each. D fell with the spells of the changed kernel, none over 10 us: an even mixture of one block a step brings the clock back. It can take longer, as the kernels with the split or the keys moved show, with spells of 17 to 20 us.

## What to carry to other kernels

Where an engine is busy all the time and the same piece of work takes 28 us here and 39 there, read the granted clock by stage before looking for waits, price it from one piece done at either level, and spread wide and narrow matmuls evenly; 28 us of useless multiplication in the thin steps made this kernel faster, and 14 us of it in the dense ones made it 31 us slower. A wait removed can be worth nothing if the order that removes it lets the clock fall: judge an order by pair time at full clock and by low clock together. And follow a moved call to every engine that it feeds, down to a one-column instruction that another engine can hold up.

## What was not expected of the hardware

- TensorE, busy in 39.22 of 39.22 us, ran at a mean clock of 0.74; with 1.8 us of idle time in 30.04 it ran at 1.00.
- A one-column operation of VectorE with two SBUF inputs took 0.96 us instead of 0.16 while GpSimd worked on a 128x1024 tile, and ended with it to 0.02 us.
- The same 14 us of matmuls moved the time by -4 us in steps 0 and 1 and by +31 us in steps 6 and 7.
- The scatter between runs of one kernel is the granted clock's: twelve runs of the kernel before go from 2762.78 us at a clock of 0.970 to 2796.67 at 0.957. That is some 75 us more at 1.2 GHz, 34 us by the price of 0.46, and 34 were measured. Twelve runs with steps 0 to 3 filled go from 2751.05 us at 0.985 to 2771.99 at 0.978.
- With one order of matmuls, a spell of low clock in pair 0 was 3 us long in some executions and 10 in others.
